# Weight tiles in eight pieces: loads that follow branch A's rounds in a hybrid RWKV-7 / retention decoder step

## The chip, the cores and the metric

The kernel runs on one core of one Trainium2 chip, as one launch. The metric is the device time of that launch in microseconds. The profile is one execution of it, taken by the hardware profiler; all stretches below are microseconds from the start of its span.

## What is computed

Two layers of a decoder trunk, for a prompt of 256 tokens and 8 sampled sequences of 8 tokens (T = 320 columns in all), D = 1024, float32:

```
h = rmsnorm(x);  z = h @ w_in                      # 1824 + 3072 + 2048 columns
ya = rwkv7(z[:, :1824])       # S_t = S w_t - (S kk_t) b_t^T + v_t k_t^T, y_t = S_t r_t, head norm, bonus, gate
yb = retention(z[:, 1824:4896])   # rotary q and k, chunked, head norm, silu gate
m = sigmoid(ga) * (ya @ w_out_a) + sigmoid(gb) * (yb @ w_out_b)
x = x + rmsnorm(m @ w_o)
h = rmsnorm(x);  f = (silu(h @ w_gate) * (h @ w_up)) @ w_down
x = x + rmsnorm(f)
```

The states of both branches and the last projected row are outputs as well.

## The kernel before

Activations lie transposed, 128 features by 320 tokens a block. A weight matrix is cut into tiles of 128 x 1024 float32 (512 KB), NT = 141 a layer, 282 in all. SP (SyncE) loads a tile into `w_raw`, ScalarE copies it to `w_hi` (L599), VectorE makes the remainder `w_lo` (L898), and TensorE multiplies three times per 128 x 128 block: high by high, low by high and high by low (L1368). Each of the three buffers is a ring of RING = 3. SP's loop `weights(n)` (L449 to L453) waits until tile n - 3 has its `w_lo`, then issues the load; its queue is strictly in order.

Branch A's recurrence is solved in chunks. For each of five streams (four chunk positions and the samples) a triangular system is inverted by doubling. This is a list of 48 rounds written out by hand, `ROUNDS` (L67): each names one or two jobs, which TensorE computes as small 64 x 64 matmuls into one of six banks and signals by `round_done`, and which VectorE or ScalarE then takes out of the bank (L1082, L1070, L732, L727). GpSimd applies some masks. Between the rounds TensorE has parts of four dense tiles to do (`PIECE_AT`: three parts each of the tiles T_V to T_V + 3, after rounds 2, 5, 8, and so on to 48), and VectorE makes a `w_lo` in four of the rounds (`LOW_AT`: in rounds 10, 18, 30 and 42, for tiles T_V + 1 to T_V + 4). Each of those frees a buffer of `w_raw`, and SP then issues the load of tile T_V + 4, T_V + 5, T_V + 6 or T_V + 7, 512 KB in one DMA. ScalarE makes `w_hi` of T_V + 4 in round 20, of T_V + 5 in round 32, of T_V + 6 after round 48 (`values`, through `high_all`), and of T_V + 7 in the sequence of chunk steps behind the rounds.

After the load of tile T_V + 7 SP does `swaps` (L459 to L466): it waits for the last VectorE operation of the rounds, loads cosine and sine into `cos_sin`, and copies `qk_raw` to `qk_rot` with its 32-row blocks exchanged, in four DMAs. GpSimd waits for these, does six of the eight rotary products (L525 to L530), decays the samples' states (L541), and does the last two. ScalarE waits for the eighth rotation before it issues the load of `dmask` (L778) and goes on with `w_hi` and the gates.

Of the kernel before, what the change touches and what calls it, by code (L numbers as in the profile page):

```python
# [21 lines left out]
T_ZA, T_QK, T_V, T_GATE, T_GAB = 0, 15, 23, 31, 39  # L22
T_WOA, T_WOB, T_WO, T_GU, T_DOWN, NT = 55, 59, 67, 75, 119, 141

G_WOA, G_WOB, G_WO, G_GU, G_DOWN, NG = 55, 63, 71, 79, 123, 131
RING, EARLY, OPEN = 3, 6, 5
# [14 lines left out]
for _n, _w in (("mix_pre", 8), ("mix_post", 8), ("ffn_pre", 8), ("ffn_post", 8), ("mu", ZA), ("w0", 4), ("a0", 4),  # L41
# [25 lines left out]
ROUNDS = ("vt0", "mt0 mx1", "mt1 mx2", "mt2 mx3", "mt3 kt0", "m0 kt1", "m1 kt2", "m2 kt3", "m3 e01", "mt4 e02", "e00 e03",  # L67
# [4 lines left out]
THIRDS = ((0, 3), (3, 6), (6, 8))  # L72
PIECE_AT = {at: (n // 3, THIRDS[n % 3]) for n, at in enumerate((2, 5, 8, 12, 16, 20, 24, 28, 32, 37, 42, 48))}
LOW_AT = {10: 1, 18: 2, 30: 3, 42: 4}
ROUND_BANKS = 6
MASKS = ("xt0", "x1", "xt1", "x2", "xt2", "x3", "xt3", "x0", "p10", "p20", "p11", "p21", "p12", "p22", "p13", "p23", "xt4", "x4",
         "p14", "k4", "b4", "kt0", "kt1", "p31", "p30", "p32", "p33", "kt2", "p41", "p40", "p42",
# [3 lines left out]
def named(text):  # L81

    name = text.rstrip("0123456789")
    ns = [int(t) for t in text[len(name):]]
    return name, ns[0] if len(ns) == 2 else 0, ns[-1]


def on_act(job):

    name, lv, s = job  # L90
    return name in ("vt", "kt", "tk", "tb") or (name == "e" and lv > 0) or (name == "m" and s in FLIP)
# [3 lines left out]
JOB_AT = {j: i + 1 for i, j in enumerate(JOBS)}  # L95
# [48 lines left out]
def program(nc, x_t, wts, pvec, lora, shift0, fixed, rmask, trig, rconst, wkv_st, ret_d, ret_t,  # L144
# [5 lines left out]
    with ctx:  # L150
        def sb(name, cols, dt=F32):
            return ctx.enter_context(nc.sbuf_tensor(name, [128, cols], dt))
# [11 lines left out]
        w_raw = [sb(f"w_raw{i}", 1024) for i in range(RING)]  # L164
# [90 lines left out]
        def many(n, *names, unit=1):  # L255

            return [Signal(name, n, unit) for name in names]
# [2 lines left out]
            ctx.enter_context(nc.semaphore(n)) for n in ("vec_loaded", "fixed_loaded", "y_stored", "pad_ready"))  # L260
        x_loaded = [ctx.enter_context(nc.semaphore(f"x_loaded{i}")) for i in range(4)]
        w_loaded = many(NT // RING, *(f"w_loaded{i}" for i in range(RING)), unit=16)
        hi_ready, = many(NT, "hi_ready")
        tile_used, = many(T_GU, "tile_used")
        low_made, = many(NT, "low_made")
# [35 lines left out]
        round_done, = many(len(JOBS), "round_done")  # L301
# [19 lines left out]
        def low_ready(layer, n):  # L321

            return low_made(layer, n + 1)

        def used(layer, n):

            if n >= T_DOWN:
                return down_used(layer, n - T_DOWN + 1)
            return tile_used(layer, n + 1) if n < T_GU else phase_done(layer, 4 * (n - T_GU + 1))
# [98 lines left out]
        def emptied(layer, job):  # L428

            name, lv, s = job  # L430
            return made(layer, job if on_act(job) else (PARTS.get(name, (name,))[-1], lv, s))
# [9 lines left out]
        def round_bank(job):  # L441

            return banks[(JOB_AT[job] - 1) % ROUND_BANKS]

        block = ctx.enter_context(nc.Block())

        @block.sync
        def _(sp):
            def weights(n):  # L449

                if n >= RING:
                    sp.wait_ge(*low_ready((n - RING) // NT, (n - RING) % NT))
                sp.dma_start(w_raw[n % RING][:, :], wts[n]).then_inc(w_loaded[n % RING].sem, 16)  # L453
            for i in range(4):
                cols = slice(2 * i * T, (2 * i + 2) * T)
                sp.dma_start(x[:, cols], x_t[:, cols]).then_inc(x_loaded[i], 16)
                if i in FIRST_WEIGHTS:
                    weights(FIRST_WEIGHTS.index(i))
            def swaps(layer):  # L459

                sp.wait_ge(*round_v(layer, len(V_OPS)))
                sp.wait_ge(*round_p(layer, len(P_OPS)))
                sp.dma_start(cos_sin[:, :], trig).then_inc(trig_loaded.sem, 16)
                for i in range(4):
                    to, of = 32 * i, 32 * (i ^ 1)
                    sp.dma_start(qk_rot[to:to + 32, :], qk_raw[of:of + 32, :]).then_inc(qk_swapped.sem, 16)  # L466

            for n in range(len(FIRST_WEIGHTS), DEPTH * NT):
                weights(n)
                if n % NT == T_V + max(LOW_AT.values()) + RING:  # L470
                    swaps(n // NT)
            for i, (lo, hi) in enumerate(X_GROUPS):
                sp.wait_ge(*x_done(DEPTH - 1, i + 1))
                sp.dma_start(y_t[:, lo * T:hi * T], x[:, lo * T:hi * T]).then_inc(y_stored, 16)
            sp.wait_ge(y_stored, 16 * len(X_GROUPS))
# [97 lines left out]
        def _(act):  # L573
# [18 lines left out]
            def high_all(upto):  # L592

                while made[0] <= min(upto, DEPTH * NT - 1):
                    n = made[0]
                    act.wait_ge(*w_loaded[n % RING](0, n // RING + 1))
                    if n >= RING:
                        act.wait_ge(*used((n - RING) // NT, (n - RING) % NT))
                    act.activation(w_hi[n % RING][:, :], w_raw[n % RING][:, :], ACT.Copy).then_inc(hi_ready.sem, 1)  # L599
                    made[0] += 1  # L600
# [9 lines left out]
            def piece(c):  # L610

                if c % 2 == 0:
                    act.wait_ge(x_loaded[c // 2], 16)
                    if c // 2 - 1 in FIRST_WEIGHTS:
                        high_all(FIRST_WEIGHTS.index(c // 2 - 1))
            open_x(0, 1, "mix_pre", piece)
            high_all(RING - 1)
            act.wait_ge(fixed_loaded, 16)
            load_consts(0)
            for layer in range(DEPTH):  # L620
                vec = vec_of(layer)

                def high(upto, base=layer * NT):
                    high_all(base + upto)
# [268 lines left out]
        def _(dve):  # L893
            def low(layer, n):

                dve.wait_ge(*hi_ready(layer, n + 1))
                r = n % RING
                dve.tensor_tensor(w_lo[r][:, :], w_raw[r][:, :], w_hi[r][:, :].bitcast(F32), ALU.subtract).then_inc(low_made.sem, 1)  # L898
# [14 lines left out]
            for layer in range(DEPTH):  # L913
# [144 lines left out]
                for i, job in ((i, named(t)) for i, slot in enumerate(ROUNDS, 1) for t in slot.split()):  # L1058
                    if i in LOW_AT and named(ROUNDS[i - 1].split()[0]) == job:
                        low(layer, T_V + LOW_AT[i])  # L1060
                    if on_act(job):
# [301 lines left out]
        def _(pe):  # L1363
            pe.wait_ge(fixed_loaded, 16)
            pe.wait_ge(pad_ready, 2)
            for layer in range(DEPTH):
# [132 lines left out]
                def need(signal):  # L1499

                    sem, value = signal
                    if waited.get(sem.name, -1) < value:
                        pe.wait_ge(sem, value)
                        waited[sem.name] = value
# [43 lines left out]
                for i, slot in enumerate(ROUNDS, 1):  # L1548
                    pair = [named(t) for t in slot.split()]
                    for job in pair:  # L1550
                        n = JOB_AT[job] - 1
                        if n >= ROUND_BANKS:
                            need(emptied(layer, JOBS[n - ROUND_BANKS]))
                        elif n == len(core):
# [402 lines left out]
```

## Time and profile before

| what | value |
| --- | --- |
| median of 3 runs | 1299.23 us (1298.85 to 1300.09) |
| the profiled execution's own time | 1297.91 us |
| its span, first to last instruction | 1296.1 us |
| TensorE busy | 1234.4 us, 95% |
| weight load of TensorE busy | 1163.6 us, 90% |
| VectorE, ScalarE, GpSimd busy | 859.7, 556.0, 157.5 us |
| mean granted clock of TensorE | 0.984 of full speed |
| DMA | 179.52 MB, mean 139 GB/s |

Busy times of the engines overlap. A share over the whole span averages stages with different limits. "Issue" in a chain is time in which an engine waited for nothing that the profile shows. The profile's line numbers are those of the kernel before.

### The profile page before, as it was taken

The numbers are of one execution on the slowest core, as the hardware profiler recorded it, in microseconds if no ns is written. First come the engines' busy times: TensorE is split into PE (matmuls) and PEld (weight loads), VectorE is DVE, ScalarE is ACT, GpSimd is POOL, SyncE is SP. The second block draws the span as 40 slices with busy tenths as digits, with TensorE's granted clock in tenths as the row PEclk, the third lists the DMA queues.
The fourth block names the chain that finished last, engine by engine and source line by source line (L and its number), as shares of the span: only waits on it lengthen the run. The fifth ranks groups of instructions, "written<-read, shape, count | busy, mean of one in ns | idle before, by whom it ended". The sixth has DMA issues, their size and how long they took to land.

```text
span 1296.1 us, 27750 instructions
## 1 busy us (share of the span) xinstructions
PE 1234.4 (95%) x11992; PEld 1163.6 (90%) x11992; DVE 859.7 (66%) x1444; ACT 556.0 (43%) x849; POOL 157.5 (12%) x168
## 2 busy tenths in 40 slices
PE   6999999899998999999899998998999989999996
PEld 5899887899998999999898987877999989999996
DVE  4887559877776665653487954787877666566433
ACT  5553334354435433343444533344444453333432
POOL 0004463300000000000000071831100000000000
PEclk9999999999999999999999999998999989999998
DMA  6333144644453545444433423255454434444441
GB/s 227 130 108 125 53 119 145 224 139 146 139 163 116 190 148 151 155 148 147 130 115 114 132 68 82 91 184 179 141 167 132 157 107 148 154 154 144 150 149 72
DMA packets 51178, 179.52 MB, mean 139 GB/s; under 512 B 6256, under 2 KB 7024, under 8 KB 49776
## 3 DMA queue, kind: packets, MB, share of 16 engines
q1 hardware_dynamic: 42576, 153.77, 37.6%
q10 hardware_dynamic: 8480, 23.97, 5.2%
q8 instruction: 95, 1.56, 0.5%
q14 instruction: 27, 0.22, 0.1%
HBM read 166.57 MB, written 8.53 MB: 135 GB/s over the span
## 4 chain that ended last, share of the span: by engine, by line
PE 83%; DVE 9%; POOL 3%; ACT 2%; issue 2%; DMA 1%; SPq 0%; ACTq 0%; DVEq 0%; POOLq 0%
PE dense L1368 51%; PE core L1368 32%; DVE w_lo L898 2%; ACT w_hi L599 1%; POOL qk_rot L530 1%; POOL rot_tmp L528 1%; POOL qk_rot L527 1%; DVE x L947 1%; DVE y_out L945 1%; DMA qk_rot<-qk_raw 1%; DMA x<-x_t 0%; POOL s_st L541 0%; DVE ya_lo L926 0%; DVE bonus L1016 0%; DVE tmp L1002 0%
## 5 line engine op out<-in xcount | busy, mean ns | idle before, releaser
L898 DVE TENSOR_TENSOR w_lo<-w_raw,w_hi 128x1024 fp32r<-128x1024 f32 x282 | 358.2, 1272 | 228.4 <-ACT w_hi L599 227.9
L599 ACT ACTIVATE w_hi<-w_raw 128x1024 fp32r<-128x1024 f32 x282 | 297.5, 1056 | 445.2 <-PE dense L1368 294.0
L1368 PE MATMUL dense<-h_hi,w_hi 128*128 128x320 f32 x1296 | 416.9, 322 | 23.4 <-DVE h_lo L902 11.8
L1368 PE MATMUL dense<-h_lo,w_hi 128*128 128x320 f32 x1296 | 404.9, 312 | 1.1 <-issue 1.1
L1368 PE MATMUL dense<-h_hi,w_lo 128*128 128x320 f32 x1296 | 404.8, 312 | 0.0
L1368 PEld LDWEIGHTS dense<-h_hi,w_hi 128*128 128x128 f32 x1296 | 247.0, 191 | 43.8 <-issue 36.9
L1368 PEld LDWEIGHTS dense<-h_lo,w_hi 128*128 128x128 f32 x1296 | 247.4, 191 | 2.7 <-issue 1.5
L1368 PEld LDWEIGHTS dense<-h_hi,w_lo 128*128 128x128 f32 x1296 | 247.4, 191 | 0.0
L1368 PE MATMUL core<-h_hi,w_hi 128*128 128x320 f32 x416 | 129.3, 311 | 0.0
L1368 PE MATMUL core<-h_lo,w_hi 128*128 128x320 f32 x416 | 128.8, 310 | 0.0
L1368 PE MATMUL core<-h_hi,w_lo 128*128 128x320 f32 x416 | 128.7, 309 | 0.0
L1368 PEld LDWEIGHTS core<-h_hi,w_hi 128*128 128x128 f32 x416 | 78.4, 188 | 0.2
L1368 PEld LDWEIGHTS core<-h_lo,w_hi 128*128 128x128 f32 x416 | 78.4, 188 | 0.2
L1368 PEld LDWEIGHTS core<-h_hi,w_lo 128*128 128x128 f32 x416 | 78.3, 188 | 0.0
L481 POOL TENSOR_TENSOR xt<-xt,fx 128x256 f32<-128x256 f32 x10 | 7.3, 732 | 564.8 <-DVE xt L1070 564.8
L587 ACT ACT_TABLE_LOAD x31 | 39.8, 1283 | 38.5 <-DMA ret_s<-ret_t 17.0
L1368 PE MATMUL dense<-f_hi,w_hi 128*128 128x320 f32 x176 | 54.2, 308 | 0.0
L1368 PE MATMUL core<-f_hi,w_lo 128*128 128x320 f32 x176 | 54.2, 308 | 0.0
L1368 PE MATMUL core<-f_hi,w_hi 128*128 128x320 f32 x176 | 54.2, 308 | 0.0
L1368 PE MATMUL dense<-f_lo,w_hi 128*128 128x320 f32 x176 | 54.2, 308 | 0.0
L1368 PE MATMUL core<-f_lo,w_hi 128*128 128x320 f32 x176 | 54.2, 308 | 0.0
L1368 PE MATMUL dense<-f_hi,w_lo 128*128 128x320 f32 x176 | 54.2, 308 | 0.0
(299 smaller groups left out, 2004.3 us busy)
## 6 DMA issues: line engine op xcount, KB each, us to landing
w_raw<-wts SPq DMA_DIRECT2D x282, 512.0 KB, 3.5
ret_t<-ret_t ACTq DMA_DIRECT2D x16, 256.0 KB, 3.8
ret_s<-ret_t ACTq DMA_DIRECT2D x16, 256.0 KB, 2.8
ret_rest<-ret_d ACTq DMA_DIRECT2D x2, 1536.0 KB, 7.5
qk_rot<-qk_raw SPq DMA_DIRECT2D x8, 320.0 KB, 6.1
dmask<-rconst ACTq DMA_DIRECT2D x2, 1152.0 KB, 5.8
s_st<-wkv_st ACTq DMA_DIRECT2D x2, 1024.0 KB, 5.0
wkv_s<-s_st ACTq DMA_DIRECT2D x2, 1024.0 KB, 7.2
```

Source lines behind the costliest of these rows:

```text
L481: return pool.tensor_tensor(pairs(t, s, C), pairs(t, s, C), bc(i2, 1, 4), ALU.add)
L527: link(pool.tensor_tensor(ch(qk_rot, i), ch(qk_rot, i), cos_sin[:, T:2 * T], ALU.mult))
L528: link(pool.tensor_tensor(rot_tmp[:, :], ch(qk_raw, i), cos_sin[:, 0:T], ALU.mult))
L530: pool.tensor_tensor(ch(qk_rot, i), ch(qk_rot, i), rot_tmp[:, :], ALU.add).then_inc(rotated.sem, 1)
L587: act.preload_act_table_set(name)
L599: act.activation(w_hi[n % RING][:, :], w_raw[n % RING][:, :], ACT.Copy).then_inc(hi_ready.sem, 1)
L898: dve.tensor_tensor(w_lo[r][:, :], w_raw[r][:, :], w_hi[r][:, :].bitcast(F32), ALU.subtract).then_inc(low_made.sem, 1)
L945: link(dve.tensor_tensor(y.rearrange("p (c t) -> p c t", t=T), y.rearrange("p (c t) -> p c t", t=T), bc(root[:, :], 1, hi - lo), ALU.mult))
L947: dve.tensor_tensor(xs, xs, y, ALU.add).then_inc(added.sem, 1)
L1368: return pe.matmul(out, lhsT, rhs, start=start, stop=stop)
```

## The change

The tiles T_V + 4 to T_V + 7 (numbers 27 to 30 of each layer) are no longer loaded by one DMA but by eight, each of 16 of the 128 partitions, 64 KB. `PACED` gives each of the four tiles the round after its `LOW_AT` round: 11, 19, 31 and 43. Ahead of piece i (0 to 6) SP waits until the first job of round `PACED + i`, at most 48, is done; the eighth piece goes out right behind the seventh. The first seven pieces count on a new semaphore of their tile, `w_part`, the eighth on the old one, and ScalarE waits for both before it copies such a tile.

```diff
--- before.py
+++ after.py
@@ -72,6 +72,7 @@
 THIRDS = ((0, 3), (3, 6), (6, 8))
 PIECE_AT = {at: (n // 3, THIRDS[n % 3]) for n, at in enumerate((2, 5, 8, 12, 16, 20, 24, 28, 32, 37, 42, 48))}
 LOW_AT = {10: 1, 18: 2, 30: 3, 42: 4}
+PACED = {T_V + RING + n: at + 1 for at, n in LOW_AT.items()}
 ROUND_BANKS = 6
 MASKS = ("xt0", "x1", "xt1", "x2", "xt2", "x3", "xt3", "x0", "p10", "p20", "p11", "p21", "p12", "p22", "p13", "p23", "xt4", "x4",
          "p14", "k4", "b4", "kt0", "kt1", "p31", "p30", "p32", "p33", "kt2", "p41", "p40", "p42",
@@ -260,6 +261,7 @@
             ctx.enter_context(nc.semaphore(n)) for n in ("vec_loaded", "fixed_loaded", "y_stored", "pad_ready"))
         x_loaded = [ctx.enter_context(nc.semaphore(f"x_loaded{i}")) for i in range(4)]
         w_loaded = many(NT // RING, *(f"w_loaded{i}" for i in range(RING)), unit=16)
+        w_part = many(7, *(f"w_part{i}" for i in range(len(PACED))), unit=16)
         hi_ready, = many(NT, "hi_ready")
         tile_used, = many(T_GU, "tile_used")
         low_made, = many(NT, "low_made")
@@ -450,6 +452,13 @@
 
                 if n >= RING:
                     sp.wait_ge(*low_ready((n - RING) // NT, (n - RING) % NT))
+                if n % NT in PACED:
+                    for i in range(7):
+                        rows = slice(16 * i, 16 * i + 16)
+                        sp.wait_ge(*round_done(n // NT, JOB_AT[named(ROUNDS[min(PACED[n % NT] - 1 + i, len(ROUNDS) - 1)].split()[0])]))
+                        sp.dma_start(w_raw[n % RING][rows, :], wts[n][rows, :]).then_inc(w_part[list(PACED).index(n % NT)].sem, 16)
+                    sp.dma_start(w_raw[n % RING][112:128, :], wts[n][112:128, :]).then_inc(w_loaded[n % RING].sem, 16)
+                    return
                 sp.dma_start(w_raw[n % RING][:, :], wts[n]).then_inc(w_loaded[n % RING].sem, 16)
             for i in range(4):
                 cols = slice(2 * i * T, (2 * i + 2) * T)
@@ -594,6 +603,8 @@
                 while made[0] <= min(upto, DEPTH * NT - 1):
                     n = made[0]
                     act.wait_ge(*w_loaded[n % RING](0, n // RING + 1))
+                    if n % NT in PACED:
+                        act.wait_ge(*w_part[list(PACED).index(n % NT)](n // NT, 7))
                     if n >= RING:
                         act.wait_ge(*used((n - RING) // NT, (n - RING) % NT))
                     act.activation(w_hi[n % RING][:, :], w_raw[n % RING][:, :], ACT.Copy).then_inc(hi_ready.sem, 1)
```

## Rows read from the trace of the kernel before

**Rows 1.** The page's chain that ended last, by engine.

```profile
PE 83%; DVE 9%; POOL 3%; ACT 2%; issue 2%; DMA 1%; SPq 0%; ACTq 0%; DVEq 0%; POOLq 0%
```

**Rows 2.** Windows: us, busy of PE, PEld, DVE, ACT, POOL, PEclk, DMA share, GB/s.

```profile
112.90:162.20 49.30, 46.11 (x1549) 41.67 (x1549) 28.27 (x65) 19.14 (x52) 29.83 (x39) 0.97 0.18 67
747.40:802.90 55.50, 46.81 (x1549) 42.08 (x1549) 27.80 (x65) 19.03 (x52) 29.90 (x39) 0.97 0.19 60
162.20:248.40 86.20, 83.08 (x1137) 71.96 (x1135) 65.62 (x110) 36.10 (x67) 43.44 (x38) 1.00 0.49 155
```

**Rows 3.** Chain in order of time, both layers' rounds: start, us, what.

```profile
149.03 2.00 issue
...
768.41 1.08 issue
...
772.65 1.15 issue
...
777.48 0.54 issue
...
785.30 2.82 issue
...
798.97 2.35 issue
```

**Rows 4.** DMA queues, windows 110:163 and 747:803: packets, MB, share of 16 engines.

```profile
q8 instruction: 12, 0.20, 1.4%
...
q8 instruction: 13, 0.21, 1.5%
```

**Rows 5.** GB/s in 40 slices, windows 148.2:149.6, 767:768.1 and 798.9:799.9.

```profile
GB/s 0 468 0 0 0 0 0 0 0 0 0 0 0 0 0 0 0 0 0 0 0 0 0 0 0 0 0 0 0 0 0 0 0 0 0 0 0 0 0 0
...
GB/s 0 0 0 0 596 0 0 0 0 0 0 0 0 0 0 0 0 0 0 0 0 0 0 0 0 0 0 0 0 0 0 0 0 0 0 0 0 0 0 0
...
GB/s 656 0 0 0 0 0 0 0 0 0 0 0 0 0 0 0 0 0 0 0 0 0 0 0 0 0 0 0 0 0 0 0 0 0 0 0 0 0 0 0
```

**Rows 6.** DMA busy tenths in 40 slices and queues, windows 783.4:785.8, then 796.7:798.9.

```profile
DMA  0099800997000408419696996969949989432010
...
q1 hardware_dynamic: 143, 0.52, 79.8%
...
DMA  0056399103323979089355997995993959939500
```

**Rows 7.** DMA queues in window 783.5:784.19, a tile's first packets.

```profile
q1 hardware_dynamic: 16, 0.07, 107.3%
```

**Rows 8.** DMA issues (KB, landing us), SP's issues (ns, when), VectorE's last.

```profile
w_raw<-wts SPq DMA_DIRECT2D x282, 512.0 KB, 3.5
...
wkv_p<-s_st ACTq DMA_DIRECT2D x2, 128.0 KB, 2.0
...
shift_o<-shift_out ACTq DMA_DIRECT2D x2, 67.5 KB, 3.0
...
L453 SPq DMA_DIRECT2D w_raw<-wts x4: 328/328/328, 759.8 to 795.9; - x4
...
L463 SPq DMA_DIRECT2D cos_sin<-trig x2: 328/328/328, 162.2 to 802.9; - x2
...
802.50 0.42 DVE L1082 TENSOR_TENSOR xt<-xt,core 128x256 f32<-128x256 f32 x1 [3.13 <-PE core L1368]
```

**Rows 9.** Waits in 206:216 and 847:858 (total, times, longest); TensorE at 855.62.

```profile
ACT w_hi L599 <- POOL qk_rot L530: 6.9, 1, 6.9
...
ACT w_hi L599 <- POOL qk_rot L530: 8.9, 1, 8.9
...
855.62 0.65 PE L1368 MATMUL core<-v_exp,tok 64*64 64x512 f32 x2 [0.65 <-DVE u_exp L1092]
```

**Rows 10.** Timeline of VectorE and ScalarE around round 17, layer 0.

```profile
131.60 0.42 DVE L1082 TENSOR_TENSOR x_sq<-x_sq,core 128x256 f32<-128x256 f32 x1 [1.20 <-PE core L1368]
...
134.16 1.06 ACT L599 ACTIVATE w_hi<-w_raw 128x1024 fp32r<-128x1024 f32 x1 [0.97 <-PE dense L1368]
```

## The prediction

> **What bounds the kernel now.** I read the page's chain first: TensorE holds 83% of the chain that ended last and "issue" only 2% [rows 1]. So a change to four loads a layer can matter only where TensorE's own work is broken, and I looked at the stretch in which those loads run, branch A's 48 rounds. The windows of the two layers' rounds are the same work (1549 matmuls each) but 49.3 us long in layer 0 and 55.5 us in layer 1, with TensorE busy 46.1 and 46.8 us [rows 2]. The reader is to see there that layer 1 loses 6.2 us over layer 0 with identical code, so neither the data dependencies nor the instruction durations explain it.
>
> The chain restricted to those windows names the loss: six stretches that it calls "issue", time in which TensorE waited for no semaphore that the profile shows: 2.00 us in layer 0; 1.08, 1.15, 0.54, 2.82 and 2.35 us in layer 1 [rows 3]. Their sum is 2.00 in the one and 7.94 in the other, and the difference, 5.94, is nearly the 6.2 us between the layers.
>
> Then the DMA view. Beside the weight loads it has a queue of kind "instruction", 12 and 13 packets in the two stretches, 0.20 and 0.21 MB, so about 16 KB each, one every 4 us or so [rows 4]. Placed by windows about 1 us wide, one such packet stands before each of the six gaps [rows 5], which have the first, the second and the last of them; the large number in a row of GB/s is the packet, in the slice in which it starts. Start of packet to end of gap: 148.25 to 151.03 (2.8 us), 767.12 to 769.49 (2.4), 771.57 to 773.80 (2.2), 775.64 to 778.02 (2.4), 785.86 to 788.12 (2.3), 798.91 to 801.32 (2.4). A gap that always ends 2.2 to 2.8 us after an instruction packet begins is TensorE waiting for its instructions. That is my reading; no row names the engine that the packet is for.
>
> Why are the four long ones long? Weight transfers run from 145.9 to 148.0, 769.1 to 771.3, 783.5 to 785.9 and 796.8 to 798.9 (read from windows like the two of [rows 6]), and the instruction packets of those gaps start 0.0 to 0.3 us after each of them ends [rows 5, 6]. In the window from 783.4 to 785.8 there are 143 packets of the weight queue and none of the instruction queue [rows 6]; the instruction packet comes as the last one ends. So a 512 KB tile, which holds all 16 DMA engines busy for 2.1 to 2.3 us, holds back whatever instruction fetch falls into it.
>
> **The change part by part.**
>
> *A, the burst goes.* Each of the four tiles a layer becomes eight DMAs of 16 rows, seven of them held by successive rounds (11 to 17, 19 to 25, 31 to 37, 43 to 48 with the last one doubled) and the eighth right behind. A fetch can then wait behind a piece but not behind a tile. The gaps tied to a transfer add to 2.00 + 1.15 + 2.82 + 2.35 = 8.32 us [rows 3]. Not all of it is the tile's: the two gaps with no transfer just ahead are 0.54 and 1.08 [rows 3], so fetches are at their limit here anyway; I leave 0.5 us in each of the four (the nearer row, 0.54), which gives 6.3. The tile issued at 759.8 lands 3.5 us later [rows 8], at 763.3, one fetch (some 4 us) ahead of the fetch of the 1.08 gap, so it can have made that earlier one late; I count half of that gap as the tile's too: 0.5 more. A = -6.8. Bounds: -8.3 - 1.08 - 0.54 = -9.9 if all six gaps close; 0 if nothing of it goes.
>
> *B, the pieces' own disturbance.* A piece is one 4 KB row to each engine if 16 rows spread as 128 do. (The Trainium skill, DMA: Bandwidth & Descriptors, "Why a DMA increments its semaphore by 16 and not by 1", has a copy of 16 partitions from SP use 16 engines; no row of before shows such a copy.) The first 16 packets of a tile had 107.3% of 16 engines in 0.69 us, so 0.74 us each [rows 7]; later ones are shorter, but in a piece every packet is a first one. A round is 49.3 / 48 = 1.03 us, so in paced rounds an engine is taken some 0.74 / 1.03 = 70% of the time, and a fetch that hits waits 0.37 on average: 0.26 us a fetch. Paced rounds are 27 of 48, so 14 of the 25 fetches: 3.6 us if none has slack. The rounds show gaps behind 6 fetches of 25 [rows 3, 4] and at least half of the fetches that are not late have room; I take half, B = +1.8. Bounds: 0, and 14 x 0.74 = +10.4 if each fetch meets a fresh piece and has no slack.
>
> *C, the SP queue ahead of the swaps.* The last tile's sixth, seventh and eighth pieces all wait for round 48. Each issue takes 0.33 us and about 0.04 to the next [rows 8], so three take 1.1 us. Before, SP issued the cosine load at 162.2 and 802.9, as soon as the last VectorE operation of the rounds (802.50, 0.42 long) was over [rows 8]. Round 48 is done about when that one starts, so the cosine load and the four swaps behind it go 1.1 - 0.45 = 0.65 us later. Behind them waits GpSimd with the rotations; ScalarE waits for the eighth rotation, 6.9 us in layer 0 and 8.9 in layer 1 [rows 9]; behind ScalarE's wait stand the mask load and the next w_hi. In layer 1 that chain reaches TensorE: the trace's critical chain passes from the swap's DMA through GpSimd, and TensorE has a 0.65 us wait at 855.62 [rows 9]. In layer 0 ScalarE's wait is 2.0 us shorter, so the rotations had that much more room, and I count the delay there as covered. So C = 0.6 in layer 1 and 0 in layer 0; bounds 0 and 2 x 1.1 = 2.2. All loads behind in the queue wait for later tiles' w_lo and are not moved.
>
> *D, the end of the first paced tile.* Its pieces end at round 17 and its w_hi is made in slot 20. VectorE takes up round 17's result at 131.60, and w_hi starts at 134.16, held by TensorE until then [rows 10]. The last piece goes out at about 131.6 + 0.37 = 131.97. From issue to landing a 512 KB tile takes 3.5 us, a 128 KB copy 2.0, a 67.5 KB one 3.0 [rows 8]. By 2.0 it lands 0.2 us before it is wanted; by 3.0, 0.8 late. Behind the waiting ScalarE are v_f, e_sq and tok, and TensorE needs the banks that they empty, so lateness would reach it. I take 0.1 a layer, D = +0.2; bounds 0 and 2 x 1.3 (3.5 us). The other three tiles have 7 rounds or more between last piece and w_hi. ScalarE's four extra waits a layer are on semaphores long reached by then; 0, and at most 8 x 0.06 = 0.5. SP's extra waits cost nothing: between 759.8 and 795.9 it issues four transfers [rows 8] and otherwise stands.
>
> Sum: -6.8 + 1.8 + 0.6 + 0.2 = -4.2 us. Nothing later swallows it: the work behind each layer's rounds (in layer 0 a window of 86.2 us with TensorE busy 83.1 [rows 2]) begins when they end, the swaps too. The profiled execution took 1297.91 us for a span of 1296.1; that gives 1293.7. The median of the runs shown is 1299.23, 1.3 us above the profiled one; against it I forecast 1295.0.
>
> The Trainium skill (Runtime: NRT & Kernel Launch, "Instruction fetch mechanics") has a rule that speaks against all of A: instructions stream in 16 KiB blocks, the next one fetched while the current one runs, and "The cost of crossing a 16 KiB boundary is one DMA tail-bump, mostly hidden". The block size agrees with 0.21 MB for 13 packets. "Hidden" does not agree with the gaps in the rounds, which end 2.2 to 2.8 us after a fetch begins. By the rule A and B would be nothing, and the time that rival 2's.
>
> **The rivals.**
>
> 1. *The pieces stand in the fetches' way (slower).* Place: rounds 11 to 48. Nearly every fetch meets a piece, since an engine is taken 70% of the time. For it: packets of a cold transfer take 0.74 us against a fetch's whole 2.2 to 2.8 us from start to resumption, and the six gaps show fetches without slack. Against it: most fetches in the rounds show no gap behind them. The kernel gets slower once B exceeds 6.8 - 0.8 = 6.0 us, 0.43 us for each of 14 fetches; measurably (2.6 us more) from 0.6 us each. At the bound of 10.4: 1299.2 - 6.8 + 10.4 + 0.8 = 1303.6. If sixteen rows went to few engines instead of sixteen, a piece would hold those longer but be met more rarely, with about the same product.
>
> 2. *The gaps are not the fetches', or were hidden anyway.* Then A and B are 0 and only C and D are left: 1299.2 + 0.8 = 1300.0. For it: the packets' engine is inferred. Against it: six gaps of six with the same distance, and the layers' unequal length.
>
> 3. *The fetches' slack is real and all six gaps go.* A = -9.9 with B about 0.5 and C + D = 0.8: 1299.2 - 8.6 = 1290.6. For it: layer 0 without its 2.00 us gap would be 47.3 us, and layer 1 brought to that gains 8.2 alone [rows 2, 3]. Against it: the 1.08 and 0.54 gaps with no transfer ahead.
>
> 4. *The saving comes back at one place:* the swaps 1.1 us late in both layers and the first tile 0.8 late in both would take 3.8 of the 5.0 that A and B leave: 1298.0. For it: there is no spare time in the rows of either place; against it: layer 0's rotations had some [rows 9].
>
> **How the numbers follow.** Forecast (a gain of 2.6 to 7 us) 0.50; rival 3 (more than 7) 0.16; rivals 2 and 4 and weak forms of the forecast, within 2.6 us either way, 0.24; rival 1 beyond that 0.10. A measurement of this kernel tells about 0.2%, 2.6 us, from no change. So faster 0.66, same 0.24, slower 0.10. The range reaches from rival 3's 1290.5 to 1300.3, past rival 2; the forecast's own part of it is 1292.2 to 1296.6.
>
> **What would show it.** A: the four "issue" stretches of 2.00, 1.15, 2.82 and 2.35 us shrink to 0.5 or less, and both windows of the rounds come near 48 to 50 us. B: "issue" stretches under 0.8 us at other places in the rounds. C: the cosine load issued about 1.1 us after the last round's matmuls instead of 0.45, and ScalarE's wait for the rotations longer than 8.9 us in layer 1. D: ScalarE's first w_hi in the rounds waiting for a DMA instead of TensorE. I am wrong if the windows of the rounds don't shorten, or if gaps of 2 us remain with only pieces in flight.

## The result: 3.7 us slower, the other way than forecast

| | median | runs | range |
| --- | --- | --- | --- |
| before | 1297.98 us | 12 | 1296.57 to 1300.09 |
| changed | 1301.72 us | 12 | 1296.76 to 1304.74 |

The ratio is 1.0031, 95% interval [1.0019, 1.0042]. That is a loss of 0.3%, small but clear of the runs' scatter. I had forecast 1295.0 us within 1290.5 to 1300.3, faster. The profiled execution of the changed kernel took 1304.74 us, its longest; its span is 1302.9 us against 1296.1, so the two profiles differ by 6.8 us where the medians differ by 3.7.

The windows of the changed kernel, in the columns of [rows 2]; the stretches run between the same operations as there (rounds of layer 0 and 1, then what lies behind each up to TensorE's 3.4 us wait). The last line is the kernel before, behind layer 1's rounds, which [rows 2] don't have:

```profile
112.90:162.20 49.30, 45.05 (x1550) 40.31 (x1550) 28.34 (x65) 18.86 (x51) 29.83 (x39) 1.00 0.20 61
756.00:806.50 50.50, 44.90 (x1550) 40.48 (x1549) 27.89 (x65) 18.85 (x51) 29.82 (x39) 1.00 0.19 60
162.20:254.90 92.70, 84.91 (x1136) 72.60 (x1134) 68.04 (x109) 36.13 (x67) 45.32 (x38) 0.98 0.48 148
806.50:896.40 89.90, 83.05 (x1134) 71.72 (x1134) 67.35 (x108) 35.48 (x67) 44.97 (x38) 1.00 0.48 152
...
802.90:889.40 86.50, 83.08 (x1137) 71.88 (x1135) 68.82 (x110) 35.87 (x67) 44.41 (x38) 1.00 0.46 155
```

Against [rows 2], layer 1's rounds went from 55.5 to 50.5 us, layer 0's stayed at 49.3, and the stretch behind layer 0's rounds went from 86.2 to 92.7 us with the same TensorE work in it. So the rounds as a whole get shorter by what was forecast, all of it in layer 1, and something behind the rounds takes more than that away.

Taken from the n-th matmul to the n-th in both traces (which avoids judging where a stretch ends), four stages in us, the two behind the rounds with TensorE's wait of 3.4 us at their end:

| kernel | rounds 0 | behind | rounds 1 | behind |
| --- | --- | --- | --- | --- |
| before | 50.2 | 89.7 | 55.6 | 90.0 |
| changed | 50.2 | 96.3 | 50.8 | 93.9 |

The rounds give back 4.9 us, the stretches behind them cost 6.6 and 3.9. (The remaining 1.3 us of the profiles' difference is scattered over the dense stages; the same stretches differ by up to 2.7 us between profiles of kernels that have the same instructions there.)

The column PEclk has a second part of the story. TensorE's granted clock was 0.97 in both layers' rounds before, and 1.00 in the changed kernel's. Two stretches of the kernel before make up that 0.97; in both the clock stood at 0.50, the lower of its two levels. The third line is the changed kernel, behind the rounds of layer 0:

```profile
151.30:154.70 3.40, 3.40 (x45) 3.07 (x49) 0.40 (x1) 0.00 (x0) 0.00 (x0) 0.50 0.02 5
789.60:793.00 3.40, 3.40 (x53) 3.07 (x56) 0.60 (x3) 0.00 (x0) 0.00 (x0) 0.50 0.00 0
...
219.60:223.00 3.40, 3.40 (x11) 1.40 (x12) 3.40 (x7) 1.01 (x3) 0.00 (x0) 0.50 0.02 5
```

Ahead of the first two TensorE had stood in the gaps of 2.00 and 2.82 us [rows 3], ahead of the third in the wait of 4.40 us that is shown below. At the lower clock the same matmuls keep TensorE busy longer: 46.11 and 46.81 us in the rounds before, 45.05 and 44.90 in the changed kernel's. That is 3.0 of the 4.9 us by which the rounds got shorter. In layer 0 it only made up for what the change cost there: the gap of 2.00 us became one of 1.45, but ScalarE waited 2.12 us for the first tile in pieces. Behind layer 0's rounds it goes the other way, 84.91 us busy against 83.08: of the 6.6 us lost there, 4.4 are the wait and 1.8 the lower clock.

What happens between the rounds and the rotations is one chain. Layer 1 of the changed kernel, in order of time (start us, us, what):

```profile
803.04 1.80 issue
804.84 1.16 PE core L1379 x42
...
806.01 1.54 SPq L459
807.55 0.04 issue
807.60 0.42 SPq L459
...
808.06 0.42 SPq L460
...
808.58 0.37 SPq L472
...
811.30 8.48 DMA qk_rot<-qk_raw
...
819.92 1.56 POOL cos_sin L534
```

TensorE ends the last round at 806.00. Then SP's queue issues the three last pieces (L459 twice, L460), the first of which takes 1.54 us, and the cosine load (L472) goes out at 808.58, 2.1 us after the last VectorE operation (2.0 in layer 0). Before, it went out 0.03 us after it. The last swap takes 8.48 us from issue to GpSimd instead of 6.52. GpSimd's first rotary operation and ScalarE's wait for the last one, changed kernel, layers 0 and 1:

```profile
176.09 1.55 POOL L534 TENSOR_TENSOR cos_sin<-cos_sin,root 128x640 f32<-128x640 f32 x1 [29.48 <-DMA qk_rot<-qk_raw]
819.92 1.55 POOL L534 TENSOR_TENSOR cos_sin<-cos_sin,root 128x640 f32<-128x640 f32 x1 [30.24 <-DMA qk_rot<-qk_raw]
```

```profile
ACT w_hi L610 <- PE dense L1379: 12.7, 1, 12.7
```

```profile
ACT w_hi L610 <- POOL qk_rot L539: 12.1, 1, 12.1
```

The last VectorE operation of the rounds ends at 162.14 and 806.44 here, so GpSimd starts 13.95 and 13.48 us after it; before, 9.68 and 10.15. ScalarE's waits answer to [rows 9]: 6.9 and 8.9 have become 12.7 and 12.1. (The profile puts the first down to TensorE, which had long been done. The mask load, which waits for the eighth rotation, is ahead of this w_hi in ScalarE's queue and went out at 212.72: it was GpSimd.)

How that reaches TensorE in layer 0, again the chain of the changed kernel:

```profile
213.18 1.06 ACT w_hi L610
...
214.26 1.28 ACT L596
...
215.93 0.46 ACT sq_a L807
...
216.88 0.69 DVE s_st L1158
...
218.89 0.61 DVE u_exp L1103
...
219.54 2.81 PE core L1379 x9
```

ScalarE, freed late, makes a w_hi, loads a table and squares; VectorE, in order, waits for that square before it may go on to s_st and u_exp; TensorE waits for u_exp, 4.40 us in layer 0 and 3.54 in layer 1 (none and 0.65 before):

```profile
219.54 1.11 PE L1379 MATMUL core<-v_exp,tok 64*64 64x512 f32 x2 [4.40 <-DVE u_exp L1103]
```

```profile
863.02 0.65 PE L1379 MATMUL core<-v_exp,tok 64*64 64x512 f32 x2 [3.54 <-DVE u_exp L1103]
```

### The profile page after: what moved, and what is told of

The parts are those of the page before. It is cut to its first block, busy times and chain, and to the rows that moved or that the text cites. A ratio compares the mean times of both kernels' runs of the same rounds, so it can differ in the third digit from the quotient of the medians.

```text
span 1302.9 us, 27822 instructions
## 1 busy us (share of the span) xinstructions
PE 1236.1 (95%) x11992; PEld 1162.9 (89%) x11992; DVE 861.7 (66%) x1444; ACT 556.3 (43%) x849; POOL 159.9 (12%) x168
## 4 chain that ended last, share of the span: by engine, by line
PE 82%; DVE 8%; ACT 3%; POOL 3%; issue 2%; DMA 1%; SPq 0%; ACTq 0%; DVEq 0%; POOLq 0%
PE dense L1379 50%; PE core L1379 31%; DVE w_lo L909 2%; ACT w_hi L610 1%; POOL qk_rot L539 1%; POOL rot_tmp L537 1%; DMA qk_rot<-qk_raw 1%; POOL qk_rot L536 1%; DVE x L958 0%; DVE y_out L956 0%; DMA x<-x_t 0%; ACT L596 0%; POOL s_st L550 0%; DVE ya_lo L937 0%; DVE bonus L1027 0%
```

## The experiments

Each was timed beside runs of the kernel before on the same chip; the ratio is against those, and 0.1% is 1.3 us. "Start" is GpSimd's first rotary operation after the end of the last VectorE operation of the rounds, layers 0 and 1 (before: 9.7 and 10.2; changed: 14.0 and 13.5). Each expectation is as it stood before the run.

**Three tiles in pieces, and the last alone.** One condition on `PACED`:

```diff
-PACED = {T_V + RING + n: at + 1 for at, n in LOW_AT.items()}
+PACED = {T_V + RING + n: at + 1 for at, n in LOW_AT.items() if n < 4}    # three; "if n == 4" for last
```

> Three of the four tiles a layer in pieces, the last one (tile 30) in one 512 KB DMA as before. Theory Q (the changed kernel is slow because the last tile's pieces push the swaps back in SP's queue, and the pieces themselves help the rounds): GpSimd's first rotary operation comes 9.6 us after the end of the rounds again, ScalarE's wait for the rotations is 7 and 9 us again, and the kernel is 3 to 6 us faster than before. Rival R (the pieces stand in the instruction fetches' way, rival 1 of the prediction): the rounds are no shorter than before and the kernel is as slow as before or slower.

> Only the last tile (tile 30) in pieces, the other three in one DMA each as before. Theory Q: the swaps land 3 to 4 us later than before in both layers, and the kernel is 4 to 8 us slower than before, about as slow as or slower than the whole change. Rival R: a quarter of the change's pieces, so at most 1 us slower.

Three: 1294.78 us, 0.9974 [0.9961, 0.9986]. Last: 1306.18 us, 1.0071 [1.0047, 1.0095]. Start with three 9.9 and 10.5, with the last alone 13.2 and 12.5. The change is a gain and a loss in one: its first three tiles alone are 3.4 us faster, its last one alone is 9.2 us slower. Rival R (pieces in the way of the fetches) expected neither.

**Almost nothing loaded in the rounds.** Pieces 0 to 6 of each tile, and ScalarE's wait for them, removed; 112 rows of these tiles are then stale data. The eighth piece, 64 KB, still goes out when the buffer is free.

> Of the four tiles only the eighth piece of 16 rows is loaded, right at the buffer's release; the other 112 rows keep what the ring buffer held, so these products are of other data. It shows the floor: no transfer of a tile in the rounds and nothing in front of the swaps. Theory F (tiles delay instruction fetches in the rounds): both windows of the rounds come to 47 to 49 us and the kernel is 7 to 10 us faster than before. Rival H (the gaps have nothing to do with the tiles' transfers): the rounds keep 49.3 and 55.5 us and the kernel is within 1 us of before.

1293.29 us, 0.9959 [0.9943, 0.9975]. The rounds take 49.2 and 50.6 us, 6.0 less than before together. The tiles' transfers do cost time in the rounds (rival H falls), but less than theory F's floor: "issue" stretches remain with no tile in flight. Its chain in the rounds, both layers:

```profile
134.95 0.81 issue
...
147.08 0.17 issue
...
149.61 1.18 issue
...
772.53 0.60 issue
...
784.50 1.49 issue
...
793.48 0.24 issue
...
795.95 1.53 issue
```

And its rounds in the columns of [rows 2]:

```profile
112.70:161.00 48.30, 44.88 (x1550) 40.24 (x1550) 28.30 (x65) 19.01 (x52) 29.89 (x39) 1.00 0.09 30
748.60:799.10 50.50, 45.59 (x1550) 40.72 (x1550) 28.26 (x65) 19.02 (x52) 29.83 (x39) 1.00 0.08 29
```

The clock stayed at 1.00, and TensorE's busy time is 1.2 us shorter than before in each layer. So of the 6.0 us only some 3.5 are shorter or absent gaps; 2.5 are the lower clock that no longer follows them.

**The last tile's pieces earlier**, two per round, in rounds 43 to 46:

```diff
-ROUNDS[min(PACED[n % NT] - 1 + i, len(ROUNDS) - 1)]
+ROUNDS[PACED[n % NT] - 1 + (i // 2 if PACED[n % NT] == 43 else i)]
```

> All four tiles in pieces, but the last tile's go two per round, in rounds 43 to 46, so that SP's queue is empty when round 48 ends. Theory Q: the swaps are issued within 0.5 us of the last VectorE operation of the rounds as before, and the kernel is 3 to 6 us faster than before, like the one with three tiles in pieces. Rival R: slower than before by 3 us as the whole change. Rival L (pieces in flight, not SP's queue, delay the swaps' data): half of the delay stays.

1301.21 us, 1.0010 [0.9993, 1.0027]: no difference that can be told, and not the 3 to 6 us hoped for. The profile says why. In layer 1 SP issued the last piece at 802.03, before the rounds' end (802.71), and the start was 10.3; in layer 0 it issued it at 162.89, after the rounds' end (161.78), and the start was 12.8. The buffer comes free at 158.6 there, eight issues at 0.46 us take 3.7, and one of them took 1.5 us. Where SP's queue was empty in time the damage was nearly gone (TensorE's wait for u_exp 1.0 us, before 0.65), with all pieces still made, so it is not the pieces' traffic; but the pace can't be had in layer 0.

**Three late DMAs alone**, and the same of 1 KB each. Of the last tile, rows 0 to 79 at once and 48 rows in three DMAs after round 48; in the second kernel everything at once but three blocks of 16 x 16 elements:

```diff
+sp.dma_start(w_raw[n % RING][0:80, :], wts[n][0:80, :]).then_inc(...)
+sp.wait_ge(*round_done(n // NT, JOB_AT[named(ROUNDS[47].split()[0])]))
+for i in (5, 6):
+    sp.dma_start(w_raw[n % RING][rows, :], wts[n][rows, :]).then_inc(...)     # tiny3: [rows, 0:16]
```

> As before, but of the last tile (30) rows 0 to 79 go out in one DMA when the buffer is free and the last 48 rows in three DMAs of 16 rows after round 48, ahead of the swaps. It isolates the three late DMAs from the paced ones. Theory Q (SP's queue ahead of the swaps is the cost): three issues of about 0.46 us put the swaps 1.4 to 2 us later, GpSimd's start after the rounds' end moves from 9.6 to 11.5 us or more, and the kernel is 2 to 5 us slower than before. Rival P (all eight pieces are needed for the damage): within 1 us of before.

> As before, but of the last tile everything except three blocks of 16 rows by 16 columns goes out when the buffer is free, in two DMAs, and the three blocks (1 KB each) after round 48, ahead of the swaps. Against late3 (same three issues, 64 KB each; 8.7 us slower). Theory Q1 (the time of three more issues in SP's queue is the cost): GpSimd starts 12 to 13.7 us after the rounds' end as in late3, and the kernel is 5 to 9 us slower. Rival Q2 (the 192 KB in front of the swaps' data are): at most half of late3's loss.

late3: 1307.0 us, 1.0069 [1.0046, 1.0093], start 12.2 and 13.8. tiny3: 1307.86 us, 1.0065 [1.0041, 1.0089], start 11.4 and 12.5. Three DMAs of 3 KB in all cost as much as three of 192 KB in all (the intervals overlap). So it is the issuing, in the main, and not the data; the start is 0.8 and 1.3 us earlier with the small ones, so the data may add a little. late3 was expected at 2 to 5 us and cost 9.0: I still priced the delay too low.

**The swaps late, with no piece at all.** The kernel before, with one wait ahead of the swaps:

```diff
 sp.wait_ge(*round_v(layer, len(V_OPS)))
 sp.wait_ge(*round_p(layer, len(P_OPS)))
+sp.wait_ge(*seq_done(layer, SEQ_AT[("u", 0)]))
```

> As before, with no piece and no additional DMA, but SP waits for TensorE's second chunk step (u of chunk 0) before it issues the cosine load and the swaps, some 3 us later than before. Theory Q (the swaps' lateness is the whole cost of the last tile's pieces): GpSimd starts 3 to 4.5 us later, TensorE waits 2 to 5 us more for u_exp in each layer, and the kernel is 5 to 9 us slower. Rival T (the pieces' traffic, or ScalarE's second wait, is what costs): at most 2 us slower.

1312.28 us, 1.0090 [1.0070, 1.0109], 11.7 us slower. SP's queue and GpSimd's start in layer 0:

```profile
165.31 0.33 SPq L464 DMA_DIRECT2D cos_sin<-trig  x1
165.68 3.87 SPq L467 DMA_DIRECT2D qk_rot<-qk_raw  x4
169.59 3.08 SPq L453 DMA_DIRECT2D w_raw<-wts  x2
```

```profile
175.84 1.55 POOL L526 TENSOR_TENSOR cos_sin<-cos_sin,root 128x640 f32<-128x640 f32 x1 [28.93 <-DMA qk_rot<-qk_raw]
```

```profile
219.29 1.12 PE L1369 MATMUL core<-v_exp,tok 64*64 64x512 f32 x2 [4.70 <-DVE u_exp L1093]
```

Late issue of the cosine load by 3.1 us, start 13.7 instead of 9.7, and nearly the same TensorE wait at the same matmul, 4.70 us. With GpSimd as late as in the change, lateness of the swaps alone reproduces its whole damage in layer 0 (the stage behind the rounds 96.6 us, the change's 96.3), with no piece and no second wait on ScalarE. This shows the mechanism from GpSimd's start on. SP is 3.1 us late here and 2.0 in the change; what adds to those 2.0 on the way to GpSimd is the next experiment's matter. In layer 1 the load is 3.1 us late too, the start is 14.3 and TensorE's wait 4.8. There the clock stood at 0.50 for 6.8 us behind the rounds, where the change had none of it, and the stage is 3.3 us longer than the change's. The loss of 11.7 us is more than the 5 to 9 I expected.

**The overlap with the next tiles.** Tile 31's load waits until the swaps have landed; put on the kernel before, on three tiles in pieces, and on the whole change:

```diff
+if n % NT == T_V + max(LOW_AT.values()) + RING + 1:
+    sp.wait_ge(*qk_swapped(n // NT, 4))
```

> As before, but SP holds the load of the next tile (31) until the four swaps have landed. Theory K (the swaps' data share the DMA engines with the 1 MB of tiles 31 and 32, which come 3 to 5 us behind them): GpSimd starts about 1 us earlier, 8.5 us after the rounds' end, and the kernel is 0 to 1.5 us faster. Rival: the landing time is the swaps' own, GpSimd starts as before at 9.6 us, and the kernel is the same or, if tile 31 is late, slower.

> Three tiles in pieces, the last in one DMA, and the load of tile 31 held until the swaps have landed. Theory K: GpSimd starts about 1 us earlier than with three tiles alone (9.8 and 10.4 us after the rounds' end) and the kernel is 4 to 6 us faster than before. Rival: as with three tiles alone, 3 to 4 us faster.

> The whole change, and the load of tile 31 held until the swaps have landed. In the change the swaps lie 3 us later but the loads of tiles 31 and 32 don't, so the two overlap more. Theory K (part of the 4.2 us by which the swaps land late is this overlap): GpSimd starts 1 to 2 us earlier than in the change (13.8 us after the rounds' end in layer 0) and the kernel is 1.5 to 3 us faster than the change, 1 to 2 us slower than before. Rival Q alone (only the time in SP's queue counts): as the change, 4 us slower than before.

hold: 1297.86 us, 0.9994 [0.9980, 1.0009], start 9.7 and 9.4: nothing in layer 0, 0.8 us in layer 1, no gain that can be told. Its rounds have the instructions of before and took as long, 49.5 and 55.2 us, but were made up otherwise: in layer 1 the long gaps were 1.71 and 2.59 us and the mean clock 0.91, with TensorE busy for 49.06 us. So how the loss divides into gaps and lower clock differs from execution to execution, and the division above is that of two profiles. three_hold: 1293.22 us, 0.9961 [0.9948, 0.9974], its interval overlaps that of three. after_hold: 1300.78 us, 1.0017 [1.0004, 1.0030], start 12.4 and 12.1 instead of 14.0 and 13.5. So of the 4.3 us by which GpSimd starts later in layer 0, 1.6 is this overlap: the swaps moved back into the loads of tiles 31 and 32, which came hardly later. By the runs it is 2.2 us slower than before where the change is 4.0, but the two intervals overlap.

**The swaps ahead of the last three pieces.**

```diff
+if i == 4 and n % NT == T_V + max(LOW_AT.values()) + RING:
+    swaps(n // NT)                  # and not behind the tile
```

> The whole change, but the swaps go out behind the last tile's fifth piece, and its last three pieces behind the swaps. Theory Q: the swaps are issued 0.05 us after the last VectorE operation of the rounds as before, GpSimd starts 9.6 to 10 us after it, the rounds are as short as in the change (50.2 and 50.8 us), and the kernel is 4 to 6 us faster than before. Rival R: within 1 us of before. Rival L (pieces in flight disturb the swaps' data): GpSimd starts 11 us or more after the rounds' end.

1302.63 us, 1.0030 [1.0017, 1.0042]: a miss. The start improved only to 11.4 and 10.3, and a new wait took the old one's place. Waits of layer 0 behind the rounds:

```profile
ACT w_hi L610 <- DMA w_raw<-wts: 7.1, 1, 7.1
```

Issues behind the swaps' data took up to 1.9 us, tile 30 landed late, ScalarE stood 7.1 us for it and TensorE 3.98 us. Two loads that are both wanted soon after the rounds can't both be last in one queue.

**Fewer pieces, or none but later.** quarters: three tiles in four pieces of 32 rows, one every second round. shifted: the kernel before, the first three tiles' single DMAs held until rounds 14, 22 and 34.

> Three of the four tiles in four pieces of 32 rows each, held by every second round; the last tile in one DMA. Theory B (a piece's issue and its cold first packets stand in the fetches' way, so fewer are better): 1 to 2 us faster than three tiles in eight pieces each (which is 3.4 us faster than before). Rival A (a longer transfer holds a fetch longer): 0 to 1 us slower than that.

> As before, but the single DMA of the first three tiles waits for rounds 14, 22 and 34, some 4 us later than before. Theory F (a gap of 1 us or more follows an instruction packet that a tile's transfer held back): the long gaps move with the transfers, each new gap over 1.5 us ends 2.2 to 2.8 us after an instruction packet that begins within 0.3 us of a transfer's end. Rival H (the gaps belong to places in TensorE's program): they stay at the same matmuls with the same lengths, 2.0, 2.8 and 2.35 us.

quarters: 1294.07 us, 0.9961 [0.9948, 0.9974], 5.1 us faster; against three alone the intervals overlap, so that fewer pieces are better stays open. shifted: 1295.73 us, 0.9974 [0.9961, 0.9987]: the same 3.4 us as three tiles in eight pieces, by moving the transfers some 2 to 5 us and cutting nothing. Its chain in layer 1's rounds, against [rows 3]:

```profile
771.00 1.12 issue
...
775.28 0.60 issue
...
783.39 0.25 issue
...
786.01 0.09 issue
...
787.26 1.21 issue
...
792.23 0.54 issue
...
796.52 0.24 issue
...
798.98 1.53 issue
```

Both theories were half right. The long gaps stay at the same matmuls, as rival H has it, but the lengths of three of them change with the transfers, as F has it: 1.15, 2.82, 2.35 became 0.60, 1.21, 1.53. (The first is as it was, 1.12 and 1.08; in layer 0 one of 2.00 became one of 1.46 and another of 1.21 appeared.) The gain is more than that:

```profile
113.30:163.00 49.70, 44.83 (x1549) 40.24 (x1550) 28.27 (x65) 19.04 (x52) 29.88 (x39) 1.00 0.20 65
750.20:802.10 51.90, 45.56 (x1549) 40.67 (x1549) 28.28 (x65) 19.00 (x52) 29.84 (x39) 1.00 0.20 62
```

The rounds are 3.2 us shorter than before together, and TensorE's busy time in them 2.5 us: in this trace most of what the shift gives in the rounds is the lower clock that did not come. Where the places of the gaps come from is seen in the kernel before, between successive gaps:

```profile
769.45:773.75 4.30, 2.80 (x126) 2.36 (x127) 1.93 (x5) 1.93 (x4) 3.44 (x5) 1.00 0.29 111
773.75:777.95 4.20, 3.67 (x126) 3.27 (x125) 1.26 (x3) 1.32 (x4) 1.47 (x3) 1.00 0.01 4
```

There are 126 matmuls and some 126 weight loads from gap to gap, and 1549 / 126 = 12.3 such groups in the rounds, which have 12 and 13 instruction packets [rows 4]. This fits a gap that can only be where one 16 KB packet's instructions end, and whose length depends on how late the next packet is. No row names the engine that a packet is for.

**Together.**

> Three tiles in four pieces of 32 rows every second round, the last in one DMA, and tile 31's load held until the swaps have landed. If the two gains add (5.1 and 0.4 to 1.6 us): 5.5 to 6.7 us faster than before. If quarters had already taken what the hold gives (no wait for the rotations left to shorten): 5 us, as quarters alone.

> No pieces: three single DMAs wait for rounds 14, 22 and 34, and tile 31's load is held until the swaps have landed. If the place of a transfer against the instruction packets is what matters (theory F), this keeps shifted's 3.5 us and adds the hold's 0.4 to 1.6: 4 to 5 us faster than before. If shifted's gain was the runs' scatter: within 1.5 us of before.

quarters_hold: 1294.27 us, 0.9950 [0.9937, 0.9964], 6.5 us faster than before on the same chip and the best ratio here (quarters alone and three_hold are within its interval). shifted_hold: 1294.52 us, 0.9958 [0.9942, 0.9975]. Both beat the kernel before and the change.

## Why the prediction was wrong, step by step

*What bounds the kernel: right as far as it went.* That the six gaps of [rows 3] are late instruction packets has stood up: taking the transfers away or moving them changed the gaps' lengths, and they sit 126 matmuls apart. What was missing is the clock. [rows 2] had 0.97 for the rounds and 1.00 behind them, and the prediction has no term for it.

*A, -6.8: the size came out, in good part by luck.* With almost nothing loaded the rounds are 6.0 us shorter. But A was made of gaps alone, and those gave some 3.5; the other 2.5 are the lower clock. I had let 0.5 us of each long gap stay; in unloaded the four are 1.18, 0.60, 1.49 and 1.53, and there is one of 0.81 us in layer 0 where there was none. In the changed kernel, with only pieces in flight, gaps of 1.45, 1.66 and 1.80 us stayed.

*B, +1.8, and D, +0.2: 1.1 together.* The change's rounds gained 4.9 against 6.0 unloaded; the runs don't tell the two apart. What B was built on didn't hold: the 0.74 us a packet were read from the first packets of one tile. A lone piece in unloaded, from 761.8 to 762.3:

```profile
q1 hardware_dynamic: 32, 0.07, 35.0%
```

Its 32 packets took 35% of 16 engines for 0.5 us, 2.8 us in all, so that its sixteen of 4 KB took at most 0.18 us each on average. D was underestimated where it starts: ScalarE waited 2.1 us for the first paced tile in layer 0 and 1.1 in layer 1:

```profile
135.22 1.06 ACT L610 ACTIVATE w_hi<-w_raw 128x1024 fp32r<-128x1024 f32 x1 [2.12 <-DMA w_raw<-wts]
```

Together A, B and D were forecast at -4.8 and the rounds measured -4.9. The sums agree; the parts don't.

*C, +0.6: the failed step.* Its words were "go 1.1 - 0.45 = 0.65 us later" and "C = 0.6 in layer 1 and 0 in layer 0". Measured: the stages behind the rounds cost 6.6 and 3.9, 10.4 us in the profile; by the runs, 9.0 for the three late DMAs alone. Five errors, the largest first:
1. The price of a late swap. I let layer 0 absorb the delay because ScalarE's wait there was 2.0 us shorter than layer 1's. The rows held no such room: TensorE's wait in layer 0 went from none to 4.40 for GpSimd 4.3 us late. GpSimd's eight rotations, ScalarE's queue, VectorE's queue and TensorE are one chain. Layer 0 has hardly any slack in it: GpSimd later by 1.7, 2.7, 3.1 and 4.0 us (tiny3, after_hold, early, swapslate) gave TensorE waits of 1.8, 3.0, 3.1 and 4.7. Only late3 shows some, 2.5 us later for a wait of 1.6. I had seen the chain in layer 1 only.
2. The swaps' landing. I counted issue time only. Late, they meet the loads of tiles 31 and 32: 1.6 and 1.4 us (after_hold).
3. The clock. Behind the long wait TensorE ran at 0.50 for a stretch, 1.8 us more of busy time in layer 0. Kernels with late swaps show this in the runs too: their mean granted clock was 0.978 to 0.980 (last, late3, tiny3, swapslate), that of the kernel before beside them 0.981 to 0.983.
4. The issue itself. I took 0.37 us a DMA from single issues; in the pieces it is 0.46, and one in the tail took 1.4 to 1.5.
5. The bound. I gave C the upper end 2 x 1.1 = 2.2, which is again the delay at SP, not what the delay can cost; rival 4 named the place at 1298.0 and got a part of 0.24.

*Rival 1 (slower)* was the wrong slower case: pieces in the fetches' way cost 1.1 us at most, not 6. Its 0.10 was all I gave to slower. *Rival 2* fell with unloaded. *The range* missed by 1.4 us above. The sign was that of one term with a wrong size.

## What to carry to other kernels

Before cutting a transfer into pieces, look at what stands behind it in the same queue: the last piece is late by design, and whatever is queued behind inherits that, multiplied by the overlap it then runs into. A delay is priced by following it to the bounding engine through every in-order queue on the way, and a term that is "covered" needs the cover's own row. Where a transfer disturbs something periodic, moving it can give what splitting gives. And the granted clock is to be read beside the gaps: here the lower clock behind the gaps cost 1.1 and 1.9 us of busy time in the two layers' rounds, beside gaps of 2.0 and 7.9.

## What the runs showed of the hardware

- Where TensorE used up 126 matmuls and as many weight loads in about 4 us, the step from one 16 KB instruction packet to the next stopped it: up to 1.5 us with no tile in flight (unloaded), up to 2.82 us behind a 512 KB transfer. The Trainium skill (Runtime: NRT & Kernel Launch, "Instruction fetch mechanics") calls this crossing mostly hidden; here it was not, and the measurement decides.
- The drops of TensorE's clock to 0.50 in the rounds stand directly behind a long gap (before: 2.00 and 2.82 us; hold: 1.73, 1.71 and 2.59), but not every long gap has one (last: none behind 1.97 and 2.86). What decides it stays open.
- SP's issue of a 64 KB piece mostly took 0.31 to 0.42 us, but up to 1.72 in the rounds. In the changed kernel's trace all nine issues there over 0.8 us overlap an instruction packet in flight (of the other 55, 14 do too). Layer 0 (count: ns min/median/max):

```profile
L459 SPq DMA_DIRECT2D w_raw<-wts x28: 310/311/1605, 125.2 to 163.1; - x28
```

  Why an issue should take longer then wasn't tried.
- A 64 KB piece lands 2.2 us after its issue, a 512 KB tile 3.5: eight times the bytes for 1.3 us more.
- The changed kernel's runs spread over 8 us, and the 12 of the kernel before beside them over 3.5. That is no mark of the change: 26 runs of the kernel before beside late3 spread over 12 us. Much of the scatter goes with the clock. Of the 86 runs of the kernel before beside the experiments, the 15 with a mean granted clock of 0.980 have a mean of 1300.5 us, the four with 0.987 one of 1295.1.
